# A two-block transformer kernel on one core: weight blocks of the expert stream taken by rows, its mixer steps laid denser, ranking by pairs of heads, and the first modulation's weights in a place of their own

## What is computed

```python
T, D = 256, 1024                      # tokens, width; two tiles of 128 tokens
for i in range(2):                    # first block
    z = x @ (mlstm_w_in[0] if i == 0 else rglru_w_in[0])      # rglru: gate 768, xr 768, xq 256 columns
    hm = mlstm_mixer(z, ...) if i == 0 else rglru_mixer(z, ...)
    ha = cross_attention(xq, mem, xattn_w_kv[i])              # 1024 x 512 weights
    mix = concat([hm, ha]) @ w_out[i]                         # 1024 x 1024
    x = layer_norm(ALPHA * x + mix, ln1_g[i], ln1_b[i])
    x = layer_norm(ALPHA * x + peer_ffn(x, ...), ln2_g[i], ln2_b[i])

def rglru_mixer(...):
    xr = conv4(xr)
    r, i = sigmoid(xr @ w_a + b_a), sigmoid(xr @ w_x + b_x)   # 8 blocks of 96
    log_a = -8 * r * softplus(-lam); a = exp(log_a)
    u = sqrt(1 - a * a) * (i * xr)
    h = scan(h * a + u)                                       # over the tokens
    return h * gelu(gate)

def peer_ffn(x, w_q, subkeys, u_tab, v_tab):                  # 8 heads, 16 experts a head and token
    s = (x @ w_q) . subkeys                                   # w_q is 1024 x 2048
    top 16 of 128 keys twice, top 16 of the 256 sums -> expert ids and softmax weights gw
    act = gelu(dot(u_tab[id], x))
    return sum over the 128 chosen experts of gw * act * v_tab[id]

mod = silu(c) @ w_ada[l] + b_ada[l]                           # 1024 x 3072, second block
```

## Time and profile before

| | us |
|---|---|
| median of 3 runs | 2532.5 (2531.1 to 2533.74) |
| the profiled execution | 2531.59 |
| its span, first to last instruction | 2529.8 |

### The profile page before, as it was taken

The page is one execution under the profiler, slowest core; times in us unless marked ns, Lnnn a source line. Parts: engine busy times, 40 slices in busy tenths (PEclk is TensorE's granted clock), DMA queues, the critical chain, the costliest instruction groups (busy, mean ns, idle before and its releaser), DMA issues. The chain is left out here.

```text
span 2529.8 us, 28560 instructions
## 1 busy us (share of the span) xinstructions
PE 2019.2 (80%) x10481; PEld 1084.4 (43%) x10481; DVE 1382.3 (55%) x3443; ACT 721.2 (29%) x2077; POOL 593.8 (23%) x529
## 2 busy tenths in 40 slices
PE   7998787556777776777686665669998999999998
PEld 5665343111443342443252111116875544886543
DVE  4556866668785457877457976442424422013433
ACT  1132422333352223363323333220014310014230
POOL 0001444444333324334333444420000000000000
PEclk8999899677998788898797788789999999999999
DMA  6646999999999999999999999984732242540431
GB/s 223 218 138 232 401 412 403 416 421 422 411 383 386 393 406 410 380 381 390 413 413 414 385 420 421 421 342 170 281 125 90 81 167 93 177 160 19 156 111 56
DMA packets 204390, 742.38 MB, mean 293 GB/s; under 512 B 26502, under 2 KB 66462, under 8 KB 138712
## 3 DMA queue, kind: packets, MB, share of 16 engines
q0 software_dynamic: 73728, 536.90, 52.2%
q1 hardware_dynamic: 117540, 199.73, 22.7%
q10 hardware_dynamic: 12984, 3.94, 0.8%
HBM read 739.39 MB, written 1.12 MB: 293 GB/s over the span
## 5 line engine op out<-in xcount | busy, mean ns | idle before, releaser
L2033 PE MATMUL psum<-expert_rows,coefs_on_diagonal 64*64 64x512 f32 x4096 | 662.1, 754 | 401.9 <-ACT coefs_on_diagonal L2452 398.8
L2632 POOL DMA_INDIRECT expert_rows<-in_peer_uv,expert_ids x512 | 589.3, 1151 | 1073.1 <-PE psum L2033 813.5
L2134 DVE SCALAR_TENSOR_TENSOR expert_rows<-expert_rows,x 128x1024 f32<-128x1024 f32 x512 | 626.0, 1225 | 380.2 <-DMA expert_rows<-in_peer_uv,expert_ids 370.7
L2033 PEld LDWEIGHTS psum<-expert_rows,coefs_on_diagonal 64*64 64x64 f32 x4096 | 143.3, 155 | 739.4 <-ACT coefs_on_diagonal L2452 547.3
L317 PE MATMUL psum<-xT,ring 128*128 128x256 f32 (+2 forms) x1472 | 323.7, 382 | 2.5 <-DMA ring<-in_mlstm_w_in 2.5
L2442 ACT ACTIVATE gelu_dots<-dots 128x2 f32<-128x2 f32 x256 | 52.1, 203 | 874.7 <-DVE expert_rows L2134 872.3
L317 PEld LDWEIGHTS psum<-xT,ring 128*128 128x128 f32 (+2 forms) x1472 | 269.3, 184 | 58.2 <-issue 11.9
L2452 ACT ACTIVATE coefs_on_diagonal<-ident,coefs 128x128 f32<-128x128 f32 x512 | 177.5, 394 | 8.3
L2445 ACT ACTIVATE coefs<-gelu_dots,gate_weights 128x1 f32<-128x1 f32 x512 | 123.0, 287 | 8.4
L3077 PE MATMUL psum<-ring,xT 128*128 128x512 f32 x256 | 122.9, 613 | 0.0
L1711 PEld LDWEIGHTS psum<-xT,ring 128*128 128x128 f32 x512 | 68.8, 213 | 64.8 <-issue 39.3
(11 more groups left out here) (427 smaller groups left out, 2169.7 us busy)
## 6 DMA issues: line engine op xcount, KB each, us to landing
ring<-in_w_in SPq DMA_DIRECT2D x64, 1024.0 KB
ring<-in_w_ada SPq DMA_DIRECT2D x24, 1024.0 KB
ring<-in_peer_w_q SPq DMA_DIRECT2D x24, 1024.0 KB
ring<-in_mlstm_w_in SPq DMA_DIRECT2D x16, 768.0 KB
ring<-in_rglru_w_in SPq DMA_DIRECT2D x16, 768.0 KB
expert_rows<-in_peer_uv,expert_ids POOLq DMA_INDIRECT x512
ring<-in_w_out_b SPq DMA_DIRECT2D x8, 1024.0 KB
ring<-in_w_o SPq DMA_DIRECT2D x8, 1024.0 KB
```

The costliest lines, as they stand in the source:

```text
L2033: last = pe.matmul(psum[64 * half:64 * half + 64, 2 * t + m, :], diag[tokens, n % DIAGS, tokens], rows[tokens, at_, D + half * 512:D + (ha ...
L2134: dve.scalar_tensor_tensor(out=rows[:, at_, 0:D], in0=rows[:, at_, 0:D], scalar=1.0, in1=x[:, n // TILE % NT, :], op0=ALU.mult, op1=ALU.mu ...
L2632: pool_.indirect_dma_start(out=rows[:, n % ROWS, :], out_offset=None, in_=table, in_offset=bass.IndirectOffsetOnAxis(ap=ids[:, at_:at_ + 1 ...
```

## The change

The stream's weight blocks of layer 1 become blocks of few rows and many columns: 512 rows (four tiles of 128) by 1024 or 768 columns, and for `w_out` two blocks of 4 x 96 rows and one of 2 x 128 rows, each 1024 columns. A product over 1024 rows then needs two blocks (three for `w_out`), and its sum stays in a PSUM bank from one to the next (`by_rows`, `block_used`); 13 ring blocks a tile become 11. The two blocks of `xattn_w_kv` become one of 512 columns. `out_products` makes 20 products of 512 columns instead of 80 of 128. The steps of the mixer are due in fewer slots (the gating chain at 41 to 51 after `at` instead of 42 to 62, the output products at 52 to 62 instead of 63 to 79, the queries from 74 instead of 94). Layer 1's tiles are ranked in chunks of two heads only. The first modulation's weights get a buffer outside the ring, refilled when `multiply` is done with it, and its own signals and banks.

```diff
+    class FirstModulation:
+        def __init__(self, layer, weights_at):
...
+            self.w = nc.alloc_sbuf_tensor_at("first_modulation_weights", [P, KD, 512], F32, offset=weights_at)
...
+        def load(self, sp, g):
+            if g:
+                sp.wait_ge(ada_summed.sem, g)
...
+        def reduce(self, pe, g):
+            pe.wait_ge(ada_summed.sem, g + 1)
+            if g >= 2:
+                pe.wait_ge(ada_added.sem, g - 1)
+            pe.matmul(psum[0:1, 6 + g % 2, :], ones[:, 0:1], self.acc[:, g % 2, :], start=True, stop=True)\
+                .then_inc(ada_reduced.sem, 1)
...
-        mod.add_weights()
+        load_after(load_mem, lambda sp: mod.load(sp, 0))
         kvj, kv_act, kv_dve = kv_jobs(layer, kmT, vm)
         qk = []
         for i in range(4):
-            mod.add_weights()
+            load_after(lambda sp, g=i + 1: mod.load(sp, g))
             qk.append(weights.add([(w, 0, P, KD)], i * 384, 384, 1))
-        mod.add_weights()
+        load_after(lambda sp: mod.load(sp, 5))
...
-        chunks = [(k, heads) for k in range(len(tiles)) for heads in (paired if k == 1 else alone)]
+        chunks = [(k, heads) for k in range(len(tiles)) for heads in (paired if k else alone)]
...
-        rk = weights.add([(a["xattn_w_kv"][1], 0, P, KD)], 0, XA_W, 1)
-        rv = weights.add([(a["xattn_w_kv"][1], 0, P, KD)], XA_W, XA_W, 1)
+        rkv = weights.add([(a["xattn_w_kv"][1], 0, P, KD)], 0, 2 * XA_W, 1)
...
-            rxq.append(weights.add([(w_mix, 0, P, KD)], 2 * RG_W, XA_W, 1))
-            rxr.append(weights.add([(w_mix, 0, P, KD)], RG_W, 384, 2))
-            rgate.append(weights.add([(w_mix, 0, P, KD)], 0, 384, 2))
-            rout.append(weights.add([(a["w_out"][1], 0, RG_B, RG_G), (a["w_out"][1], RG_W, P, 2)], 0, 256, 4))
-            rq.append([weights.add([(a["peer_w_q"][1], 0, P, KD)], c * 512, 512, 1) for c in range(PE_H // 2)])
+            rxr.append([by_rows(w_mix, i * D // 2, P, 4, RG_W, RG_W + XA_W) for i in range(2)])
+            rgate.append([by_rows(w_mix, i * D // 2, P, 4, 0, RG_W) for i in range(2)])
+            rout.append([by_rows(a["w_out"][1], 0, RG_B, 4, 0, D), by_rows(a["w_out"][1], 4 * RG_B, RG_B, 4, 0, D),
+                         by_rows(a["w_out"][1], RG_W, P, 2, 0, D)])
+            rq.append([by_rows(a["peer_w_q"][1], i * D // 2, P, 4, c * D, D) for c in range(2) for i in range(2)])
...
         def query_made(k, h):
-            return base_of(k - 1) + 94 + 3 * h + 3
+            return base_of(k - 1) + (81, 84, 92, 95)[h // 2]
...
+                    ins = pe.matmul(outs[name][0:wide, c * P:(c + 1) * P], w[:, kt, col:col + wide],
+                                    xT[:, i * run.ktiles + kt, t * P:(t + 1) * P],
+                                    start=i == 0 and c == 0 and kt == 0, stop=last_of)
...
+            def block_used(ins, n, left):
+                if left < 2:
+                    ins.then_inc(half_done[1 - left].sem, 1)
+                elif left < 4:
+                    ins.then_inc(bank_read[n % RING][3 - left].sem, 1)
...
+                        ins = pe.matmul(outs[half][:, :], left, w[0:left.shape[0], kt, half * 512:(half + 1) * 512],
+                                        start=i == 0 and kt == 0, stop=last_part and kt == 1)
...
-                    yield at + 63
-                    yield from paced(out_products(t), at + 63, 5)
-                    yield at + 82
+                    yield at + 52
+                    yield from paced(out_products(t), at + 52, 2)
+                    yield at + 62
                     spread_rows(2 * t + 3, slice(0, 3))
```

More of the change, by code:

```diff
@@ L11 @@
 from contextlib import contextmanager
+from itertools import islice
 import concourse.bass as bass
@@ L1027, in mlstm_layer @@
         assert place[0] <= early
-        mod = Modulation(layer // 2 * 2)
+        assert place[0] - weights_at >= KD * 512 * 4
+        mod = FirstModulation(layer // 2 * 2, weights_at)
         bg = a["mlstm_b_gates"][layer // 2]
@@ L1035, in mlstm_layer, with load_after, small @@
         rg = weights.add([(w, 0, P, KD)], 4 * ML_W, 2 * ML_H + XA_W, 1)
-        weights.small_loads = load_mem
-        mod.add_weights()
+        def load_after(*loads):
+            def small(sp):
+                for load_ in loads:
+                    load_(sp)
+            weights.small_loads = small
+        load_after(load_mem, lambda sp: mod.load(sp, 0))
         kvj, kv_act, kv_dve = kv_jobs(layer, kmT, vm)
@@ L1717, in pair_queries, with queries @@
+            def block_used(ins, n, left):
[3 more added lines that the diff above has]
+                    ins.then_inc(bank_read[n % RING][3 - left].sem, 1)
+            def queries(k, c):
+                for i in range(2):
+                    yield from by_rows(rq[k][2 * c + i], i, 2,
+                                       [(("q", k, 2 * c + j), [512 * j + b * P for b in range(4)]) for j in range(2)], k - 1)
             def pair_queries(c, t, blocks=(0, 1, 2, 3), name=None):
@@ L1929, in beside @@
[L1929 to L1939 removed]
+                    block = inputs(t)
```

396 lines of the change are left out of this document (208 added, 188 removed).

## The result

| | before | changed |
|---|---|---|
| median, us | 2531.3 (2528.9 to 2533.7, 7 runs) | 2540.3 (2533.0 to 2543.8, 7 runs) |
| span of the profiled execution | 2529.8 | 2531.2 |

The ratio is 1.0034, with a 95% interval of 1.0021 to 1.0047. The forecast of 2513 and its range of 2494 to 2526 are missed, and the sign too: what was the rival with a chance of 0.08, the gating chain that dries the gathers up, is what happened. The profiled execution of the changed kernel is the fastest of its seven. A second measurement of the same kernel gave 2539.7 us (2538.5 to 2546.6, 5 runs), ratio 1.0047 (1.0030 to 1.0063); its profiled execution had a span of 2536.7 and shows the same picture with larger holes.

What follows compares the result with a forecast made beforehand. DMA bounds the stream: bytes of gathers and weights times price, plus starved places. 2531.6 - 14 (packets) - 6.6 (ranking) + 4 (denser mixer) - 2.5 (first modulation) = 2512.5, with 0.9 for the median 2513; range 2494 to 2526.

Steps and rivals of the forecast that it cites:

- the gating chain that dries the gathers up: Rival, chance 0.08: VectorE's three waits for ScalarE put it 20 us behind, places stand empty; costs 35 us, 2548 or 2545.
- What bounds the kernel: Stream's 1451 us are bytes of gathers and weights times their price, plus few places where the DMA engines starve.
- The denser mixer: Gating chain, slots 43 to 51: VectorE falls 20 us behind, mostly covered; +4 us for both tiles, bounds 0 and +35.
- The waits: VectorE's new waits for ScalarE in the gating chain: 4.2 us for `r_ready`, 5.3 for decays, 5.4 for `i_ready`, 15 in all.
- The cover: Some seven gathers under way or landed, worth 17 to 21 us, hide VectorE's lag; weights fill holes if a slot is free.
- The row that I took for nearest: Tile boundary inside layer 1's half: 40 us in which VectorE never waits for a transfer cost 3.8 us.
- Packets: Longer packets for the stream's weights cut their DMA time: 14 us saved, between 10.6 (surcharge by bytes) and 25.8.
- surcharge by packets: Rival, chance 0.17: extra cost of `w_out`'s 96 rows goes with packet count, so 26 us saved instead of 14; 2501.
- Ranking: Layer 1's two tile boundaries: with pairs both DMA gaps go, -6.6 us; bounds 0 and -6.6.
- First modulation: First stage: TensorE's 1.89 us wait for a bank goes and weights come earlier; -2.5 us, bounds -4 and +1.
- long rows gain nothing: Rival, chance 0.06: DMA engines are bound by something the same for all packet lengths, so no 14 us; 2527.

Runs made afterwards that it cites:

- the other version: Changed kernel with VectorE's gating-chain steps and everything from the output products on two slots later: 2517.1 us, ratio 0.9949 to the kernel before; again 2513.4 us, 0.9942.

## Why the prediction was wrong

**What bounds the kernel**: right. The differences in the stream are bytes times price or holes in the DMA share; beside them only the time of the first gather moved.

**The denser mixer**: here the forecast broke, at +4 us where the holes took 21 and undoing the dense chain gave back 22.6. Two steps of that paragraph failed.

- The waits. I put down 15 us for three waits on ScalarE, and they are 13.4 (4.7, 4.3 and 4.4 for 4.2, 5.3 and 5.4). But I had looked only at steps that ScalarE feeds. The division of the cross attention, at 42 and now at 41, waits for TensorE's product, which moved from slot 38 to 40, so that four slots of distance became one, and stands behind a pair that this very dot completes: 7.1 to 10.5 us, some 8 us of the time. Moved steps must be checked by distance from their cause on every engine, not by kind.
- The cover. I let the DMA engines need 3.0 us a slot with weights beside them throughout, so 27 for nine slots, and seven rows of cover. But `w_out` is through at 728 us, the ring is full until its products run, and from then on a gather needs 2.5 us while VectorE takes 5. The condition that I wrote down, that weights fill a hole if the ring has a free slot, was the right one, and I didn't check it: the order of issues and the slot of the first output product would have told.

The row that I took for nearest, the boundary, where 40 us without a wait cost 3.8, was no measure: there VectorE was busy for 19 of 20 us and dots went on; here it stood still for half of 40 us. The rival had the mechanism, the place and the sign, but counted three waits where there are four, and its price of 35 us is 12 too high where mine was 19 too low.

**Packets**: 14 us forecast, 5.7 and 8.7 measured in the active time of the changed kernel's two profiles, 7.9 in the mean of all. The line in the time of a packet held: 2.454 and 2.506 estimated, 2.47 and 2.55 measured. The mis-sized term is `w_out`'s 96 rows. I had bounds of 15.4 and 30.6 us and leaned a little from the upper one; it stayed at 6.29 x 5.3 = 33.3, outside both. The surcharge isn't added to a packet's price, by byte or by packet; 96 rows have a price of their own near 5.3, and with that the sum gives 129.4 - 88.2 - 33.3 = 7.9. My bound for a surcharge by packets was itself wrong: with a quarter of the packets 2.41 / 4 = 0.60 us a MB would be left, 19.2 us for the part and 22.0 saved, not 15.4 and 25.8. It changes nothing here. The Trainium skill, "SBUF — State Buffer", "Door 1: The DMA port swizzle", has partitions 0 to 63 on even ports and 64 to 127 on odd ones, so that 96 rows load half of the ports twice as much, which goes by bytes. The traces agree in so far as the price of a MB doesn't fall with the packet's length; but the factor of 4/3 worked out from the page, an estimate, would make it 3.3 us a MB and 20.6 us, and measured is 5.3 / 2.46 = 2.2 at equal packets.

**Ranking**: both gaps went, as said. 6.6 forecast; 2.3 alone, and 3 to 7 in the other version.

**First modulation**: the wait of 1.89 us went and TensorE was through 5 us earlier; forecast -2.5, by itself -0.6 at the end, within the bounds given. The first gather comes 4.1 us earlier in the changed kernel's profile; what I had not asked is whether this is still there at the end.

**Rivals**: that long rows gain nothing is refuted at 128 rows by 2.64 against 2.47; at 96 rows it is what happened. Without the dense chain, the change is worth 13.9 to 15.7 us, where my other terms added to 23.1.

**Readings of mine that were off.** 140 us x 1.011 / 58.82 MB is 2.41, not 2.38; what I used throughout, 2.376, is within 0.2% of 140 / 58.82 without the factor. The DMA digit is 9 for 22 slices. The eight ScalarE operations of 0.37 us overlap and take 2.1 us together, as the same row says. The earlier trace rows don't show TensorE at its fullest: in the kernel before it was busy for all of 730 to 740 us (granted clock 0.86). None of these carries the forecast. The dry rival with 14 us for packets is 2544, not 2545.

## What to carry to other kernels

A step that waits for another engine belongs at least one full round of that engine behind the work that sets its cause off. If the other engine looks for work once in two slots, this means the next pair; two slots of distance, with the steps behind them moved along, were worth 23 us here, at no cost in work. In a loop that is bound by transfers, a stall of the consumer is free only as long as something else is ready to flow: look whether the queue of other loads has a free buffer at that time before calling it covered. And price a transfer by its shape over the partitions first, by its packet length second.

## What the runs showed of the hardware

- Loads into 96 partitions beside gathers cost 5.1 to 5.5 us a MB at packets of 1, 2 and 4 KB, loads into 128 partitions 2.9, 2.6 and 2.46 (what is left of the time when gathers count 2.376). Both queues suffer: with 96 rows under way a gather's packet of 8 KB took 0.753 x 40 x 16 / 1348 = 0.357 us of an engine, with 128 rows of the same length 0.657 x 20 x 16 / 751 = 0.280.
- Packet price goes on falling above 2 KB: 2.64, 2.55, 2.47, 2.38 us a MB at 2, 3, 4 and 8 KB.
- TensorE's granted clock differs from one profile to the next in the same stretch. From 150 to 170 us it is 1.00, 0.91, 0.83 or 0.74, where in the 20 us before TensorE was busy for 19.5 us or more at 1.00. From its first product of the attention to the first gather it takes 107.6 to 107.9 us at 1.00 throughout (eight profiles), 109.0 with the 0.91 and 110.9 to 114.0 with 0.83 or 0.74 (five).
